# Rotary halves of the second mixer: exchanged by transfers within the on-chip memory instead of a product with a permutation matrix

## The chip, the cores and the metric

One Trainium2 chip, one core. The metric is the device time of the whole kernel in microseconds, as the median of several executions. TensorE multiplies matrices from the on-chip memory (SBUF) into the accumulator memory (PSUM, eight banks); VectorE (DVE), ScalarE (ACT) and GpSimd (POOL) work elementwise; SyncE (SP) and ScalarE issue transfers.

## The reference, cut to what matters

Three transformer blocks on 512 tokens of width 1024. The middle one's mixer has two halves that both start from the same normed input: a state space scan (16 heads in chunks) and a differential attention (8 heads of two 64-wide score maps each). The attention's queries and keys are turned by a rotary embedding before the scores:

```python
def rope(x, pos):                       # x: (batch, tokens, 16 heads, 64)
    half = x.shape[-1] // 2
    inv_freq = 10000.0 ** (-jnp.arange(half) * (2.0 / x.shape[-1]))
    ang = pos[:, :, None] * inv_freq
    cos, sin = jnp.cos(ang)[:, :, None, :], jnp.sin(ang)[:, :, None, :]
    x1, x2 = x[..., :half], x[..., half:]
    return jnp.concatenate([x1 * cos - x2 * sin, x2 * cos + x1 * sin], axis=-1)

def diff_attention_group(q, k, v, pos, layer, lambdas, subln):
    q, k = rope(q, pos), rope(k, pos)
    ...
        p1 = masked_softmax(q1 @ k1.T * scale, mask)
        p2 = masked_softmax(q2 @ k2.T * scale, mask)
        return (p1 - lam * p2) @ v
```

The third block's attention has a rotary part 32 wide, done in the same manner with its own matrix; it stays as it is but for the numbers of its semaphores.

## The kernel before, in words

Everything is laid out with features on the 128 partitions and the 512 tokens along the free dimension. Each engine runs one program in the order in which it is written; the engines meet by semaphores. Weights stream in panels of 128x1024 through five buffers: SP loads a panel, ScalarE casts it to its high part (`hi_to`, L1296), GpSimd subtracts to get the low part (L588), and TensorE multiplies in three rounded products for each pair of 128-row tiles (`units`, L617 to L619; 8 such steps make a projected tile 128x512).

The attention's queries and keys are projected in four parts p = 0 to 3, each of four tiles (`dqk0` to `dqk3`, tile n goes to `QD[p][:, n, :]`) and a value panel (`dv0` to `dv3`). Each tile holds two 64-wide heads, so its partitions are four groups of 32: first half, second half, first half, second half. ScalarE copies a finished tile out of its bank (`copy_dqkv`, L1566). TensorE then multiplies it by the matrix `rot64`, which exchanges the groups in pairs and changes the sign of one of each (`rotate`, L908, full fp32, into bank 2). VectorE does `rope` in three operations: bank 2 times the sine table (L2264), the tile times the cosine table (L2266), and their sum (L2267).

None of this is a stage by itself. The projection is filling that TensorE does between the steps of two other loops:

- the scan, 32 steps (`SSM_FILL`): in step s TensorE does half of the filling, the decay terms of step s + 1 (`segments`, L935 and L937, into banks 4 and 5), the other half, then the output products of step s (L958). `segments(s + 1)` waits until ScalarE's exponentials of step s (L1580) have read the banks. VectorE multiplies the exponentials by the masked products (L2295). In every fourth step VectorE also gates the output (`gate_y`, L2277 and L2280) or splits it into rounded parts (`split_y`, L1856, L1857, L1862). Parts 0 and 1 are projected here.
- the attention, 32 steps (`DIFF_FILL`): scores of step c + 1 (`scores`, L978, and the mask, L966) wait until the exponentials of step c (L1600) have read their banks; the exponentials wait for the maxima (L2310, L2311); probabilities are scaled (L2344 to L2347) and turned (L1022). Parts 2 and 3 and the first output projection (`out2a`) are projected here.

The patterns say how many fill steps TensorE takes in each loop step, a `rotate` counting as one. `steps_done` works out from the same numbers in which loop step a tile is finished (`DONE_SSM`, `DONE_DIFF`); ScalarE and VectorE use those tables to place their copies and rotations. In loop step s ScalarE does the exponentials of s (in the attention they were done in the step before) and then copies the tiles finished in step s - 1, casts a panel, and goes on to the exponentials of the next step; VectorE does its products of step s, then `gate_y` or `split_y`, then the rotations of the tiles listed for step s - 1. In the attention, VectorE does the rotations before the maxima of step s + 1.

Of the kernel before, what the change touches and what calls it, by code (L numbers as in the profile page):

```python
# [15 lines left out]
P = 128  # L16
# [119 lines left out]
for _name, _n in LATE:  # L136
# [2 lines left out]
NL = _at  # L139

CONSTS = [
    ("ident", 128), ("ones", 128), ("after", 128), ("upto", 128), ("rot64", 128), ("rot32", 128),
    ("pool_inv", 64), ("eps", 1), ("freq64", 1), ("freq32", 1),
]
CCOL = {}
_at = 0
# [24 lines left out]
def constants():  # L171

    i = np.arange(P)
    c = {}
    c["ident"] = np.eye(P)
    c["ones"] = np.ones((P, P))
    c["after"] = (i[:, None] > i[None, :]) * 1.0
    c["upto"] = (i[:, None] <= i[None, :]) * 1.0
    c["neg_keep"] = (i[:, None] >= i[None, :]) * -BIG
    c["neg_future"] = (i[:, None] > i[None, :]) * -BIG  # L180
    c["chunk_rows"] = ((i[:, None] % 64 == 63) & (i[None, :] < 64)) * 1.0
    rot = np.zeros((P, P))
    for m in range(P):
        rot[m + 32 if m % 64 < 32 else m - 32, m] = -1.0 if m % 64 < 32 else 1.0
    c["rot64"] = rot
    rot = np.zeros((P, P))
    for m in range(P):
        rot[m + 16 if m % 32 < 16 else m - 16, m] = -1.0 if m % 32 < 16 else 1.0
    c["rot32"] = rot
    pos = np.arange(1, 17)  # L190
    c["pool_inv"] = np.tile(np.concatenate([1.0 / np.minimum(pos, w) for w in POOL_W]), (P, 1))
    c["eps"] = np.full((P, 1), EPS)
    f64 = (10000.0 ** (-np.arange(32, dtype=np.float32) * np.float32(2.0 / 64)).astype(np.float64)).astype(np.float32)
    f32 = (10000.0 ** (-np.arange(16, dtype=np.float32) * np.float32(2.0 / 32)).astype(np.float64)).astype(np.float32)
    c["freq64"] = np.tile(f64, 4)[:, None]
    c["freq32"] = np.tile(f32, 8)[:, None]
    c["head"] = (i[:, None] == 32 * np.arange(4)[None, :]) * 1.0
    c["pick"] = ((i[:, None] % 32 == np.arange(16)[None, :]) & (i[:, None] < 96)) * 1.0
    return [np.concatenate([np.asarray(c[n], np.float32) for n, _ in names], axis=1) for names in (CONSTS, MASKS)]
# [56 lines left out]
def build(nc, xt, weights, vectors, late, consts, masks, w_gates, positions, out):  # L256

    ctx = ExitStack()
    with ctx:
# [192 lines left out]
        def lvec(name, i=0, n=1):  # L452
# [45 lines left out]
        s_zin, s_zs = sem("z_ready_for_silu"), sem("z_silu_ready")  # L498
        s_par, s_parx = sem("params_a"), sem("params_b")
        s_ang, s_sin = sem("angles_ready"), sem("sines_ready")  # L500
        s_qc, s_vd, s_rot, s_rotf, s_roped = (sem("qk_copied"), sem("v_copied"), sem("rotated"), sem("rotated_read"),
                                              sem("roped"))
        s_sc, s_mx, s_ex, s_pn, s_tr, s_pt, s_dv, s_osq, s_os, s_or, s_osp, s_og, s_yb = (
# [27 lines left out]

        def dqkv_items(p):
            name = f"dqk{p}"
            return [((name, 0), 8), ((name, 1), 8), (("rot", 4 * p), 1), ((name, 2), 8), (("rot", 4 * p + 1), 1),
                    ((name, 3), 8), (("rot", 4 * p + 2), 1), (("part", p), 12), (("rot", 4 * p + 3), 1),
                    ((f"dv{p}", 0), 4)]

        SSM_FILL = (3, 3, 3, 4)
        DONE_SSM = steps_done(dqkv_items(0) + dqkv_items(1), SSM_FILL, 32)
        DIFF_FILL = (12,) + (4, 5, 5, 5) * 7 + (5, 5, 5)  # L540
        _items = dqkv_items(2)
        _items.insert(1, (("cols", 0), 0))
        _items.insert(3, (("spread", 0), 0))
# [57 lines left out]
        def _(pe):  # L601
# [298 lines left out]
            products_bc(6)  # L900
            products_bc(7)

            def rotate(i):
                p, n = divmod(i, 4)
                pe.wait_ge(s_qc, i + 1)
                if i >= 1:
                    pe.wait_ge(s_rotf, i)
                mm_(ps[:, 2, :], con("rot64"), QD[p][:, n, :], start=True, stop=True).then_inc(s_rot, 1)  # L908

            def fill_dqkv(p):  # L910
                for n in range(4):
                    yield from units((f"dqk{p}", n), HX)
                    if p == 2 and n == 0:
                        norm_cols("gate", 7)
                    if p == 2 and n == 1:
                        norm_spread("gate", 7, RTG)
                    if n:
                        rotate(4 * p + n - 1)
                        yield
                for u, _ in enumerate(token_units((f"dv{p}", 0), HX)):  # L920
                    yield
                    if u == 11:
                        rotate(4 * p + 3)
                        yield

            def segments(s):
                pair, i = divmod(s, 4)
# [218 lines left out]

            def rotate_mla(i):
                if i:
                    pe.wait_ge(s_rotf, 16 + i)
                    pe.wait_ge(s_qc, 16 + i)  # L1150
                else:
                    pe.wait_ge(s_od, 6)
                    pe.wait_ge(bank_free[3], uses_through(3, "od_in"))
                mm_(ps[:, 3, :], con("rot32"), QR[:, i - 1, :] if i else OD[:, 9, :], start=True, stop=True
                    ).then_inc(s_rot, 1)

            def regroup(m):

                pe.wait_ge(s_gelu, m + 1)
                if m:  # L1160
                    pe.wait_ge(s_gs, 4 + m)
                else:
                    pe.wait_ge(s_rotf, 16 + 3)
                for i in range(TAPS):
                    for q in range(4):
                        mm = mm_(ps[32 * q:32 * q + 32, 3, CH * i:CH * i + CH], con("ident")[:, 32 * i:32 * i + 32],
                                 UU[:, 4 * m + q, :], start=True, stop=True)
                mm.then_inc(s_regrouped, 1)
# [118 lines left out]
        def _(act):  # L1287
# [260 lines left out]
            for c in range(6, 8):  # L1548
                copy_bc(c)

            def copy_dqkv(tile):
                name, t = tile
                if name in ("rot", "part", "spread"):
# [10 lines left out]
                if name == f"dqk{p}":  # L1564
                    bank = USE[tile][0][0]
                    link(nc.scalar.copy(QD[p][:, t, :], ps[:, bank, :]))  # L1566
                    act.sem_inc(bank_free[bank], 1)
                    act.sem_inc(s_qc, 1)
                else:
                    copy_rows(tile, lambda q: VD[p][:, q, :], s_vd)  # L1570
                hi_to(last_panel(name, t) + 5)
# [265 lines left out]
        def _(dve):  # L1837
# [410 lines left out]
            for t in range(8):  # L2248
# [5 lines left out]
                if t == 5:  # L2254
                    dve.wait_ge(s_sin, 1)
                    cosine(COS)
                    link(v.tensor_tensor(COS, COS, R, ALU.mult))
                    link(v.tensor_tensor(SIN, SIN, R, ALU.mult))

            def rope(i):  # L2260
                p, n = divmod(i, 4)
                x = QD[p][:, n, :]
                dve.wait_ge(s_rot, i + 1)
                link(v.tensor_tensor(ROPE_T, ps[:, 2, :], SIN, ALU.mult))  # L2264
                dve.sem_inc(s_rotf, 1)
                link(v.tensor_tensor(x, x, COS, ALU.mult))  # L2266
                link(v.tensor_tensor(x, x, ROPE_T, ALU.add))  # L2267
                dve.sem_inc(s_roped, 1)

            def ropes(tiles):  # L2270
# [240 lines left out]
            def rope_mla(i):  # L2511
                x = QR[:, i - 1, :] if i else OD[:, 9, :]
                tmp = S5T[0]
                dve.wait_ge(s_rot, 16 + i + 1)
                link(v.tensor_tensor(tmp, ps[:, 3, :], SINM, ALU.mult))
                dve.sem_inc(s_rotf, 1)
                link(v.tensor_tensor(x, x, COSM, ALU.mult))
# [252 lines left out]
```

## Time and profile before

| | us |
|---|---|
| median of three executions (2553.76 to 2554.94) | 2554.46 |
| the profiled execution, its own time | 2556.53 |
| span of its records | 2554.7 |
| TensorE busy | 2469.6 (97%) |
| VectorE busy | 1296.2 (51%) |
| GpSimd busy | 1061.4 (42%) |
| ScalarE busy | 868.2 (34%) |

The span runs from the first to the last record of the profiled execution; 1.8 us lie around it. Shares are means over stages with different limits. A busy TensorE is not one at its peak: matmuls are pipelined and their records overlap.

### The profile page before, as it was taken

Reading aid. Unit: us, or ns where it says so; the run is one execution under the profiler, and the core shown is the slowest. Engines: PE = TensorE matmul, PEld = TensorE weight load, DVE = VectorE, ACT = ScalarE, POOL = GpSimd, SP = SyncE. Lnnn points to the kernel's source line nnn. Section 1 sums busy time; section 2 is a strip of 40 time slices with the busy share of each in tenths; the row PEclk is TensorE's granted clock in tenths of the full one; section 3 lists DMA queues with packets and bytes.
Section 4 is the critical chain, followed back from the end, with each engine's and each line's share of the span. In section 5 each row is a group of like instructions: output and inputs, shape, how many; then the busy total and the mean of one; then the engine's idle time right before and its main releaser. Section 6 shows DMA issues by size and latency. Waiting matters only on the chain.

```text
span 2554.7 us, 30093 instructions
## 1 busy us (share of the span) xinstructions
PE 2469.6 (97%) x11694; PEld 1976.1 (77%) x11694; DVE 1296.2 (51%) x1928; ACT 868.2 (34%) x1360; POOL 1061.4 (42%) x830
## 2 busy tenths in 40 slices
PE   8999999999999999999989999999999889999998
PEld 6877667888888888876767778888888756788886
DVE  6336687533633321585757655586126865533301
ACT  4453246222322222244444433322224353322221
POOL 4323244654544445353222245455453222544442
PEclk9999999999999999999999999999998999999999
DMA  4212122322332333221111123332331112222232
GB/s 147 69 56 77 62 72 87 99 93 89 111 96 94 99 94 96 95 79 58 50 50 50 50 74 106 99 99 90 97 98 51 31 34 64 98 99 92 95 98 78
DMA packets 62573, 209.44 MB, mean 82 GB/s; under 512 B 6880, under 2 KB 9184, under 8 KB 62304
## 3 DMA queue, kind: packets, MB, share of 16 engines
q1 hardware_dynamic: 61424, 204.11, 25.0%
q10 hardware_dynamic: 1008, 3.41, 0.4%
q8 instruction: 93, 1.52, 0.2%
q14 instruction: 48, 0.39, 0.0%
HBM read 205.39 MB, written 2.10 MB: 81 GB/s over the span
## 4 chain that ended last, share of the span: by engine, by line
PE 86%; DVE 10%; ACT 2%; issue 2%; DMA 0%; DVEq 0%; ACTq 0%; SPq 0%
PE ps L617 24%; PE ps L619 24%; PE ps L618 24%; DVE T L2163 1%; PE ps L638 1%; PE ps L639 1%; PE ps L640 1%; PE ps L958 1%; PE ps L734 1%; ACT A L1600 1%; PE ps L725 1%; PE ps L991 1%; PE ps L978 1%; PE ps L812 1%; DVE small L2310 1%
## 5 line engine op out<-in xcount | busy, mean ns | idle before, releaser
L588 POOL TENSOR_TENSOR w_lo<-w_raw,w_hi 128x512 fp32r<-128x512 f32 (+4 forms) x822 | 1051.6, 1303 | 1454.9 <-ACT w_hi L1296 1454.7
L617 PE MATMUL ps<-H,w_hi 128*128 128x512 f32 x1880 | 756.5, 402 | 22.6 <-DVEq L1858 11.7
L619 PE MATMUL ps<-H,w_lo 128*128 128x512 f32 x1880 | 738.0, 393 | 0.0
L618 PE MATMUL ps<-H,w_hi 128*128 128x512 f32 x1880 | 737.2, 392 | 0.0
L1296 ACT CAST w_hi<-w_raw 128x1024 fp32r<-128x1024 f32 (+4 forms) x411 | 402.9, 984 | 523.7 <-DMA w_raw<-in_weights_dram 517.4
L617 PEld LDWEIGHTS ps<-H,w_hi 128*128 128x128 f32 x1880 | 356.1, 189 | 115.6 <-issue 24.4
L617 PE MATMUL ps<-split,w_hi 128*128 128x512 f32 x1034 | 411.5, 398 | 6.8 <-issue 3.3
L619 PEld LDWEIGHTS ps<-H,w_lo 128*128 128x128 f32 x1880 | 355.7, 189 | 75.8
L618 PEld LDWEIGHTS ps<-H,w_hi 128*128 128x128 f32 x1880 | 356.3, 190 | 73.2 <-issue 2.6
L619 PE MATMUL ps<-split,w_lo 128*128 128x512 f32 x1034 | 403.7, 390 | 0.0
L618 PE MATMUL ps<-split,w_hi 128*128 128x512 f32 x1034 | 403.5, 390 | 0.0
L1881 DVE TENSOR_TENSOR T<-ps,R 128x512 f32<-128x512 f32 x164 | 113.4, 691 | 411.7 <-PE ps L619 407.2
L617 PEld LDWEIGHTS ps<-split,w_hi 128*128 128x128 f32 x1034 | 194.5, 188 | 55.5 <-issue 11.7
L619 PEld LDWEIGHTS ps<-split,w_lo 128*128 128x128 f32 x1034 | 194.5, 188 | 40.9
L618 PEld LDWEIGHTS ps<-split,w_hi 128*128 128x128 f32 x1034 | 194.7, 188 | 40.3 <-issue 1.7
L1888 DVE TENSOR_TENSOR X<-X,ps 128x512 f32<-128x512 f32 x48 | 33.0, 687 | 332.4 <-PE ps L619 330.8
L1310 ACT ACTIVATE SQ<-X 128x512 f32<-128x512 f32 x49 | 31.0, 632 | 211.3 <-DVEq L1890 198.6
L1483 ACT ACTIVATE T<-T 128x512 f32<-128x512 f32 x66 | 41.7, 632 | 170.9 <-DVEq L2130 170.9
L2133 DVE TENSOR_TENSOR T<-T 128x512 f32<-128x512 f32 x66 | 78.3, 1186 | 9.7
L638 PE MATMUL ps<-w_hi,H 128*128 128x256 f32 x256 | 78.3, 306 | 0.0
L639 PE MATMUL ps<-w_lo,H 128*128 128x256 f32 x256 | 72.4, 283 | 0.0
L640 PE MATMUL ps<-w_hi,H 128*128 128x256 f32 x256 | 72.2, 282 | 0.0
(405 smaller groups left out, 2401.1 us busy)
## 6 DMA issues: line engine op xcount, KB each, us to landing
w_raw<-in_weights_dram SPq DMA_DIRECT2D x323, 512.0 KB, 3.5
w_raw<-in_weights_dram SPq DMA_DIRECT2D x48, 448.0 KB, 3.2
w_raw<-in_weights_dram SPq DMA_DIRECT2D x22, 256.0 KB, 2.6
X<-in_xt_dram SPq DMA_DIRECT2D x4, 512.0 KB, 7.8
out_dram<-A SPq DMA_DIRECT2D x8, 256.0 KB, 2.1
w_raw<-in_weights_dram SPq DMA_DIRECT2D x12, 128.0 KB, 2.0
w_raw<-in_weights_dram SPq DMA_DIRECT2D x6, 192.0 KB, 2.3
A<-in_w_gates_dram ACTq DMA_DIRECT2D x1, 1024.0 KB, 4.9
```

The lines of the kernel that those rows point to most:

```text
L588: sub = nc.gpsimd.tensor_tensor(w_lo[:, p % NS, c], w_raw[:, p % NS, c], w_hi[:, p % NS, c].bitcast(F32), ALU.subtract)
L617: mm_(ps[:, bank, :], r(wh), xh, start=(k == 0), stop=False)
L618: mm_(ps[:, bank, :], r(wh), xl, start=False, stop=False)
L619: mm = mm_(ps[:, bank, :], r(wl), xh, start=False, stop=(k == kt - 1))
L638: mm_(o, xh, r(wh), start=(k == 0), stop=False)
L639: mm_(o, xh, r(wl), start=False, stop=False)
L640: mm = mm_(o, xl, r(wh), start=False, stop=(k == kt - 1))
L1296: nc.scalar.copy(w_hi[:, p % NS, 0:PSIZE[p]], w_raw[:, p % NS, 0:PSIZE[p]]).then_inc(w_hi_ready[p % NS], 1)
L1483: A_(T[:, j % 2, :], T[:, j % 2, :], ACT.Silu).then_inc(s_silu, 1)
L1881: link(v.tensor_tensor(dst, ps[:, bank, :], R, ALU.mult))
L1888: link(v.tensor_tensor(X[:, t, :], X[:, t, :], ps[:, bank, :], ALU.add))
L2133: link(v.tensor_tensor(T[:, 2 + q, :], T[:, 2 + q, :], T[:, q, :], ALU.mult))
```

## The change

The matrix `rot64` and the sixteen products are taken out. When ScalarE has copied tile i = 4p + n, it issues four transfers within the on-chip memory, each of 32 partitions by 512 tokens (64 KB), which write the tile with its halves exchanged into ROPE_T. Before, it waits until VectorE has finished `rope` of the tile before (`s_swapf`), because there is one ROPE_T. The sign goes into the sine table by a column of plus and minus one (`sign64`). `rope` waits for the four transfers instead of the product, and multiplies ROPE_T by the sine table in place. A rotation no longer counts as a fill step: both patterns are cut by one fill step in each fourth loop step, eight in all in each loop.

```diff
-            return [((name, 0), 8), ((name, 1), 8), (("rot", 4 * p), 1), ((name, 2), 8), (("rot", 4 * p + 1), 1),
-                    ((name, 3), 8), (("rot", 4 * p + 2), 1), (("part", p), 12), (("rot", 4 * p + 3), 1),
+            return [((name, 0), 8), ((name, 1), 8), (("rot", 4 * p), 0), ((name, 2), 8), (("rot", 4 * p + 1), 0),
+                    ((name, 3), 8), (("rot", 4 * p + 2), 0), (("part", p), 12), (("rot", 4 * p + 3), 0),
                     ((f"dv{p}", 0), 4)]
 
-        SSM_FILL = (3, 3, 3, 4)
+        SSM_FILL = (3, 3, 3, 3)
...
-        DIFF_FILL = (12,) + (4, 5, 5, 5) * 7 + (5, 5, 5)
+        DIFF_FILL = (12,) + (4, 5, 5, 4) * 7 + (5, 5, 4)
...
-            def rotate(i):
-                p, n = divmod(i, 4)
-                pe.wait_ge(s_qc, i + 1)
-                if i >= 1:
-                    pe.wait_ge(s_rotf, i)
-                mm_(ps[:, 2, :], con("rot64"), QD[p][:, n, :], start=True, stop=True).then_inc(s_rot, 1)
...
+            def swap_halves(p, t):
+                if p or t:
+                    act.wait_ge(s_swapf, 4 * p + t)
+                else:
+                    act.wait_ge(s_dtn, 1)
+                    act.wait_ge(s_csr, 1)
+                for b in range(4):
+                    other = 32 * (b ^ 1)
+                    act.dma_start(ROPE_T[32 * b:32 * b + 32, :], QD[p][other:other + 32, t, :]).then_inc(s_swap, 16)
+
             def copy_dqkv(tile):
...
                     link(nc.scalar.copy(QD[p][:, t, :], ps[:, bank, :]))
                     act.sem_inc(bank_free[bank], 1)
                     act.sem_inc(s_qc, 1)
+                    swap_halves(p, t)
...
-                    link(v.tensor_tensor(SIN, SIN, R, ALU.mult))
+                    link(v.scalar_tensor_tensor(SIN, SIN, con("sign64"), R, ALU.mult, ALU.mult))
...
             def rope(i):
                 p, n = divmod(i, 4)
                 x = QD[p][:, n, :]
-                dve.wait_ge(s_rot, i + 1)
-                link(v.tensor_tensor(ROPE_T, ps[:, 2, :], SIN, ALU.mult))
-                dve.sem_inc(s_rotf, 1)
+                dve.wait_ge(s_swap, 64 * i + 64)
+                link(v.tensor_tensor(ROPE_T, ROPE_T, SIN, ALU.mult))
                 link(v.tensor_tensor(x, x, COS, ALU.mult))
                 link(v.tensor_tensor(x, x, ROPE_T, ALU.add))
+                dve.sem_inc(s_swapf, 1)
                 dve.sem_inc(s_roped, 1)
```

`fill_dqkv` on TensorE loses its calls of `rotate` and the fill steps they made. The waits of the third block's rotation are renumbered, since `s_rot` and `s_rotf` now start at zero there.

## Rows read from the trace of the kernel before

**Rows 1.** The page: busy time by engine, share of the span, instructions.
```profile
PE 2469.6 (97%) x11694; PEld 1976.1 (77%) x11694; DVE 1296.2 (51%) x1928; ACT 868.2 (34%) x1360; POOL 1061.4 (42%) x830
```

**Rows 2.** Windows: scan, attention; stretch, length, five engines' busy time, clock, DMA.
```profile
1165.00:1286.00 121.00, 118.62 (x635) 81.22 (x633) 75.97 (x120) 55.44 (x100) 31.43 (x23) 1.00 0.15 49
...
1296.00:1420.00 124.00, 114.96 (x640) 87.46 (x640) 78.08 (x177) 58.12 (x142) 26.71 (x20) 0.96 0.14 43
```

**Rows 3.** Waits of TensorE: sum, times, longest; then single ones in brackets.
```profile
PEld ps L908 <- ACTq L1568: 1.6, 2, 0.8
...
1299.05 0.70 PE L978 MATMUL ps<-A 64*128 64x256 f32 x4 [3.03 <-ACTq L1602]
...
1321.75 0.49 PE L978 MATMUL ps<-A 64*128 64x128 f32 x4 [1.38 <-ACTq L1602]
...
1398.68 0.70 PE L978 MATMUL ps<-A 64*128 64x256 f32 x4 [1.88 <-ACTq L1602]
```

**Rows 4.** Records by line, ns min/median/max; two fp32 products, a rounded one, on the chain.
```profile
L908 PE MATMUL ps<-A,C_ x32: 590/592/1061, 1188.7 to 1419.2; 128*128 128x512 f32 x32
...
L2267 DVE TENSOR_TENSOR A<-A x16: 691/694/1704, 1194.2 to 1424.1; 128x512 f32<-128x512 f32 x16
...
1158.28 0.86 PE ps L889 x2
1159.14 0.23 PE ps L617
```

**Rows 5.** Timeline of the scan: exponentials, a cast, a subtraction, a rotation; start, duration.
```profile
1190.14 0.84 ACT L1580 ACTIVATE T<-ps,small 128x256 f32<-128x256 f32 x2 [0.50 <-PE ps L937]
...
1197.84 1.26 ACT L1580 ACTIVATE T<-ps,small 128x512 f32<-128x512 f32 x2 [3.51 <-PE ps L937]
...
1205.12 0.84 ACT L1580 ACTIVATE T<-ps,small 128x256 f32<-128x256 f32 x2 [2.75 <-PE ps L937]
...
1208.63 0.62 ACT L1580 ACTIVATE T<-ps,small 128x128 f32<-128x128 f32 x2 [1.40 <-PE ps L937]
...
1210.31 1.05 ACT L1296 CAST w_hi<-w_raw 128x1024 fp32r<-128x1024 f32 x1 [0.18 <-ACT A L1566]
...
1211.43 3.02 POOL L588 TENSOR_TENSOR w_lo<-w_raw,w_hi 128x512 fp32r<-128x512 f32 x2 [7.31 <-ACT w_hi L1296]
...
1211.75 0.69 DVE L2264 TENSOR_TENSOR A<-ps,A 128x512 f32<-128x512 f32 x1
...
1216.28 1.05 ACT L1580 ACTIVATE T<-ps,small 128x384 f32<-128x384 f32 x2 [2.06 <-PE ps L937]
```

**Rows 6.** Timeline: issues on ScalarE's queue; SP's loads, us to landing.
```profile
8.25 0.33 ACTq L1330 DMA_DIRECT2D C_<-in_consts_dram  x1
8.62 0.45 ACTq L1331 DMA_DIRECT2D A<-in_masks_dram  x1
...
9.20 0.63 ACT L1306 ACTIVATE ACC<-X 128x512 f32<-128x512 f32 x1
...
DMA to landing us min/median/max: 1.9/3.4/12.6
```

**Rows 7.** Timeline of the attention: steps 1 and 6.
```profile
1311.92 1.28 ACT L1557 ACT_TABLE_LOAD   x1
...
1313.65 0.58 ACT L1600 ACTIVATE A<-ps,small 128x384 f32<-128x384 f32 x1 [0.44 <-DVE small L2311]
...
1340.35 0.68 DVE L2264 TENSOR_TENSOR A<-ps,A 128x512 f32<-128x512 f32 x1
...
1345.37 0.69 ACT L1600 ACTIVATE A<-ps,small 128x512 f32<-128x512 f32 x1 [3.89 <-DVE small L2311]
```

**Rows 8.** Windows of TensorE: stretch, length, busy (records), granted clock, DMA share, GB/s.
```profile
1300.00:1308.00 8.00, 8.00 (x26) 0.57 0.20 66
1399.00:1404.00 5.00, 5.00 (x20) 0.66 0.37 110
1321.00:1330.00 9.00, 7.33 (x37) 1.00 0.19 58
```

## What the change does to the time: the prediction

> **What bounds the kernel now.** I read the page's totals first [rows 1]. TensorE is busy 97% of the span, VectorE 51%, ScalarE 34%. So work taken off TensorE is worth its own length where the engine never waits, and nothing where it already waits for somebody. Both things are found in the stage that the change touches, so I read it in stretches [rows 2]. In the scan (1165 to 1286 us) TensorE is busy 118.6 of 121 us. In the attention (1296 to 1420) it is busy 115.0 of 124, and its long waits there are for ScalarE's exponentials: 3.0, 1.4, 1.9 us [rows 3]. The reader should keep the two apart: the scan is bound by TensorE, the attention alternately by TensorE and by the round maxima (VectorE), exponentials (ScalarE), next scores (TensorE).
>
> **What is removed.** Sixteen products of 128x128 by 128x512 in full fp32, two records each. They overlap with neighbours, so the mean of one record (0.59 us) overstates them and I take the row of the chain in which two such records in a row hold 0.86 us [rows 4]. Bounds: 0.46 us if they went at the pace of the rounded products (0.23 us each in the same view), 1.18 us by two means. 16 x 0.86 = 13.8 us, half in the scan (6.9), half in the attention (6.9). With them go two waits for the copy of a tile, 1.6 us, in the scan [rows 3]. The patterns of filling lose one step a head there, as many as there were products, so no projection work is moved between engines; the last tiles of each part move at most one step.
>
> VectorE: the first of the three operations of `rope` read one operand from PSUM, in 0.69 us [rows 5]; the third, with both from SBUF, has a median of 0.69 and a maximum of 1.70 [rows 4], the latter where GpSimd was subtracting (in step 11 from 1211.43 to 1214.45 [rows 5]). Alone, the first stays what it was: three operations and the gaps between them are 2.25 us. Beside a subtraction it may now take 1 us more. (The Trainium skill, "SBUF — State Buffer", Who interferes with whom, says so: a two-input operation of VectorE with both inputs in SBUF contends with GpSimd's reads, and one with a single SBUF input doesn't. The trace agrees, 1.70 against 0.69.) The sign moved into the sine table swaps one operation for another of the same size, once: nothing.
>
> **What is added, and where.** ScalarE's queue gets, right behind the copy of each of the sixteen tiles, a wait and four transfers. Two prices.
>
> First, issuing. The rows that are nearest are ScalarE's own: two transfers were issued at 8.25 and 8.62 us, durations 0.33 and 0.45, and the next activation came at 9.20 [rows 6]. That is 0.33 us bare and 0.37 to 0.47 from one to the next. Both are of 128 rows, none of 32 within the on-chip memory; below, the price could be near nothing if the number of rows sets it; above it is 4 x 0.47 = 1.9 us. I take the nearest row, a little over its bare duration, as the cost of an instruction and not of bytes: 4 x 0.39 = 1.55 us for each tile, 25 us of ScalarE in all. The question is what they push. [...]
>
> Second, the wait. The one buffer ROPE_T is free only when `rope` of the tile before is over, and VectorE does that `rope` in the same step as ScalarE copies the tile (the schedule puts both at the step in which the tile is complete). So ScalarE, which used to go straight from the copy to the cast of the next weight panel, stands until VectorE has done its products of this step and the whole rotation. Behind it in the queue are the cast (1.05 us) and the exponentials of the next step, for which TensorE waits: `segments(s + 2)` may not overwrite its bank before exponentials s + 1 have read it.
>
> Scan, tile 3 of a part (step 11, and 27), from the start of its exponentials at 1208.63 [rows 5]. VectorE: products and `split_y`, then `rope` from 3.12 (1211.75); it takes 2.25 us to 5.37, since GpSimd's subtraction comes after the cast and so is later now. ScalarE: wait over at 5.45, four issues 7.0, cast 8.15, then the first exponential, 0.63: 8.8. TensorE wants that bank when? Exponentials s + 2 began at 1216.28, so 7.65 after; less the product that is gone (0.86) and 0.4 for the segment itself: 6.4. It waits 2.4 us.
> Tile 1 (step 6, and 22), from 1190.14 [rows 5]: `rope` starts at 1.35, ends 3.6, issues to 5.25, cast to 6.4, a square of 0.63, first exponential 7.4. Wanted at 7.7 - 0.69 (one unit less in the pattern) - 0.4 = 6.6: 0.8 us.
> Tile 2 (step 8, and 24), from 1197.84: `rope` 2.05 to 4.3, issues 5.95, cast 7.1, exponential 7.65; wanted at 7.28 - 0.17 - 0.4 = 6.7: 0.95 us.
> Tile 0 has no wait, since the `rope` before is long over; its 1.55 us fit into the 2 us that ScalarE idles there: nothing.
> Sum for two parts: 2 x (2.4 + 0.8 + 0.95) = 8.3 us, and 0.8 for products of VectorE that now meet GpSimd's subtraction (an estimate: of six such places nearly one is longer by 1.0 us, the maximum less the median in [rows 4]). Scan: -6.9 - 1.6 + 8.3 + 0.8 = +0.6 us.
>
> Attention. Here the wait itself is free: the maxima of the next step come behind the same `rope` on VectorE, and ScalarE's exponentials wait for them anyway. What is not free is that issues and cast, which ran beside the rotation, now follow it. Step 6 [rows 7]: `rope` began at 1340.35 and, with GpSimd beside it, the maxima let the exponentials go at 1345.37. Now `rope` ends at 1342.6 (no subtraction yet), the issues at 1344.25, the cast at 1345.4: even. Step 1 has no rotation but two table loads behind the cast, the last over at 1313.20; with the issues at 1314.75, so that the exponentials start 1.1 us later than at 1313.65. Gone through in the same way, tile 1 (whose `rope` moves a step forward) is 0.3 us later, tile 2 0.3, and the second part's four cancel: 1.7 us. Against it stand the eight products. Six of them (0.86 us each) lie in rounds whose length VectorE and ScalarE set, and turn into waiting; two, among the value filling of each part, are in steps where TensorE never waits: 1.7 us gained. Attention: 0.0.
>
> Landing is hidden: 1.9 us at least, 3.4 in the median from issue to landing [rows 6], and 4.4 us or more lie between a tile's last issue and its `rope` (least for tile 2 of the last part, whose `rope` comes in the very next step). Without that cover each microsecond late would be one of VectorE.
>
> **The clock.** The waits also cost afterwards. TensorE stood 3.0 us before 1299.05, and over the eight us from 1300 the mean granted clock was 0.57 (1.2 of 2.4 GHz for most of it): 8 x 0.43 = 3.4 us lost [rows 3, 8]. After 1.88 us of waiting before 1398.7 it was 0.66 over five us: 1.7 us. After 1.38 us before 1321.75 it stayed at 1.00. By my sums four new stands of 1.9 us or more arise (2.4 us for tile 3 of both parts of the scan; some 3 us in steps 2 and 6 of the attention, where the wait before 1321.75 and one of 1.0 us take up the delays and the product's time). If half of them bring the lower level at the mean price of 2.5 us: +5.0 us.
>
> Sum: +0.6 + 0.0 + 5.0 = **+5.6 us**. The profiled execution took 2556.5 (span 2554.7 and 1.8 around it), 2.1 above the median of 2554.46; so 2562.1 for a profiled one, **2560.1 us** by the median.
>
> **Rivals.**
> A, the forecast: holds at ScalarE eat the saving and some clock is lost; 2556 to 2566.
> B, no change: the same holds, but no new drop of the clock, 2554.5 + 0.6 = 2555.1. For it: 1.38 us left the clock alone; against it: 1.88 did not.
> C, faster: issues on ScalarE cost little. By the lower bound, near nothing, each tile's hold shrinks by up to 1.55 us: the scan's stalls become 0, 0 and 0.85, twice, 1.7 us, and 6.9 + 1.6 - 1.7 = 6.8 is gained; in the attention the delays go and up to four products' time stays, 3.4: together -10.2, 2544.3 us, with no drop of the clock. It decides from under about 0.15 us for an issue. Against it stand the issue rows, though none has this shape. [...]
> D, much slower: a shape of 32 rows costs more to issue (0.8 us each would add 1.6 us to each of some ten exposed tiles, +16, with the clock 2576), or landings come behind `rope`.
>
> **Numbers.** A measurement of this kernel can tell 0.2%, 5.1 us. Chances: A 0.45, B 0.20, C 0.17, D 0.18. Faster is C, 0.17. A lies around the line of 2559.6; two thirds of it, and D, are slower: 0.48. The rest, 0.35, is same. The range leaves out the far halves of C and D: 2548 to 2573; A's own is 2556 to 2566.
>
> **What would show it.** Right: ScalarE issues 64 transfers of about 0.35 us; the four of a tile start within 0.2 us of the end of the third operation of `rope`; in the scan new waits of TensorE at the segments' weight loads for the exponentials, some 8 us in six, the longest at steps 12 and 28; in the attention the waits at L978 for the exponentials grow by the products' time, with waits of 3 us in steps 2 and 6. Wrong: issues of 0.1 us (then C); no waits at the segments (ScalarE had more slack than I count); a `rope` that waits for its transfer; a clock without new drops (B).

## The result, and the profile after

| | before | after |
|---|---|---|
| median, us (four executions each) | 2554.11 | 2578.05 (2574.24 to 2582.54) |
| ratio | | 1.0107 [1.0088, 1.0127] |
| ratio, the change run again (e12_again) | | 1.0107 [1.0089, 1.0124] |
| the profiled execution, its own time | 2556.53 | 2574.24 |
| first output product of the scan to the first scores | 118.3 | 140.5 |
| first scores to the last product of `root_spread` | 208.4 | 215.3 |
| from there to the end | 1055.1 | 1046.3 |

The change makes the kernel slower by 1.1%. I had forecast 2560.1 us with a range to 2573; it ended 5 us above the range. The last three rows of the table cut the profiled execution into stretches. Of the 17.7 us between the two spans (2554.7 and 2572.4) the scan has +22.2 and the attention +6.9. What lies ahead of the scan is 2.6 us shorter, which is within its scatter: that stretch is all but the same work in the fourteen profiles of this study and ends at 1170.3 to 1177.5 us. The stretch behind the attention is 8.8 us shorter; nothing ties that to the change, see the last section.

The page after, busy time by engine and the shares of the chain; TensorE's share fell by one point [rows 1], and an issuing line is on the chain with 1% of the span.

```profile
PE 2461.3 (96%) x11662; PEld 1971.9 (77%) x11662; DVE 1302.6 (51%) x1928; ACT 866.5 (34%) x1360; POOL 1059.4 (41%) x830
...
PE ps L615 23%; PE ps L617 23%; PE ps L616 23%; ACTq L1544 1%; DVE T L2159 1%; ACT A L1596 1%; PE ps L636 1%; DVE T L2291 1%; PE ps L637 1%; PE ps L638 1%; PE ps L732 1%; PE ps L723 1%; DVE small L2306 1%; PE ps L757 1%; PE ps L810 1%
```

The line of the new transfers (L1544): duration of an issue in ns, smallest, median and largest, then issue to landing.

```profile
L1544 ACTq DMA_DIRECT2D A<-A x64: 514/612/616, 1177.8 to 1431.2; - x64
...
DMA to landing us min/median/max: 1.9/2.0/3.0
```

An issue holds ScalarE's queue for 0.61 us, where I had taken 0.39 (ScalarE's earlier ones were 0.33 and 0.45 [rows 6]). Landing is hidden, as forecast.

The same two stretches of windows as in [rows 2], and the waits of the scan and the attention (sum, times, longest):

```profile
1165.00:1286.00 121.00, 106.97 (x527) 72.65 (x527) 70.68 (x104) 46.48 (x86) 27.96 (x20) 0.93 0.20 59
...
1296.00:1420.00 124.00, 107.77 (x593) 82.74 (x594) 71.39 (x155) 52.78 (x125) 26.27 (x20) 0.94 0.20 60
```
```profile
ACT w_hi L1281 <- issue: 39.3, 8, 7.1
...
PEld ps L919 <- ACT T L1576: 16.9, 7, 4.6
...
PEld ps L962 <- ACTq L1598: 18.0, 14, 4.9
```

In the scan TensorE is busy 107.0 of 121 us where it was 118.6, and the clock is 0.93 where it was 1.00. Ahead of the segments (L919) it waits 16.9 us for ScalarE's exponentials (L1576); before there was no such wait. ScalarE in turn is held eight times ahead of a cast (L1281), 4.9 us in the mean, wait and issues together. (A stand of TensorE is counted in two ways below: "PEld" at the weight load ahead of the segments, which gives the sums and the longest, and "PE" at the product behind it, up to 0.5 us less, which gives the single ones.)

Tile 3 of the first part, which is step 11 of [rows 5], in the timeline after (ScalarE, VectorE, TensorE; start, duration, in brackets the idle time before):

```profile
1211.04 0.60 ACT L1576 ACTIVATE T<-ps,small 128x128 f32<-128x128 f32 x2
1211.92 0.59 ACT L1561 COPY A<-ps 128x512 f32<-128x512 f32 x1 [0.27 <-PE ps L617]
...
1214.14 0.69 DVE L2260 TENSOR_TENSOR A<-A 128x512 f32<-128x512 f32 x1
...
1215.59 0.69 DVE L2262 TENSOR_TENSOR A<-A 128x512 f32<-128x512 f32 x1
...
1216.37 2.44 ACTq L1544 DMA_DIRECT2D A<-A  x4
1218.85 1.04 ACT L1281 CAST w_hi<-w_raw 128x1024 fp32r<-128x1024 f32 x1 [6.35 <-issue]
...
1220.54 0.69 PE L919 MATMUL ps<-CS,CR 80*128 80x384 f32 x1 [3.06 <-ACT T L1576]
```

Read it downwards. ScalarE's copy is over at 1212.51. It then stands until `rope` of the tile before ends at 1216.28, issues from 1216.37 to 1218.81, casts to 1219.89, and only then does the exponential for which TensorE has stood 3.06 us. This is the forecast order of events; the forecast stand was 2.4. `rope` itself is here as fast as foreseen, 0.69 us for its first and third operation.

The clock of TensorE in windows of 4 us across three of the six stands (stretch, length, busy, granted clock, DMA share, GB/s):

```profile
1192.00:1196.00 4.00, 2.59 (x12) 0.95 0.26 64
1196.00:1200.00 4.00, 4.00 (x15) 0.63 0.00 0
...
1216.00:1220.00 4.00, 1.48 (x12) 0.93 0.27 66
1220.00:1224.00 4.00, 3.46 (x15) 0.50 0.00 0
1224.00:1228.00 4.00, 4.00 (x20) 0.71 0.00 0
...
1272.00:1276.00 4.00, 0.04 (x1) 0.76 0.27 66
1276.00:1280.00 4.00, 3.83 (x12) 0.50 0.00 0
```

With four of the six stands come 3 to 7 us at 1.2 GHz (a window of 0.50 is all at that level, one of 0.71 more than half of it); those that end at 1206.12 and 1264.54, of 1.74 and 1.21 us, have none. The fall can begin while TensorE still stands: it resumes at 1276.17, and the window up to 1276 already has 0.76. Over the whole scan of 140.5 us the granted clock is 0.91. That is up to 140.5 x 0.09 = 12.6 us lost, an upper bound, since a part of the low level lies in the stands themselves.

### The profile page after: what moved, and what is told of

Same layout as the page of the kernel before. It is cut to its first block, busy times and chain, and to the rows that moved or that the text cites. A ratio compares the mean times of both kernels' runs of the same rounds, so it can differ in the third digit from the quotient of the medians.

```text
span 2572.4 us, 30079 instructions
## 1 busy us (share of the span) xinstructions
PE 2461.3 (96%) x11662; PEld 1971.9 (77%) x11662; DVE 1302.6 (51%) x1928; ACT 866.5 (34%) x1360; POOL 1059.4 (41%) x830
## 4 chain that ended last, share of the span: by engine, by line
PE 80%; DVE 13%; ACT 3%; issue 2%; ACTq 2%; DMA 0%; DVEq 0%; SPq 0%
PE ps L615 23%; PE ps L617 23%; PE ps L616 23%; ACTq L1544 1%; DVE T L2159 1%; ACT A L1596 1%; PE ps L636 1%; DVE T L2291 1%; PE ps L637 1%; PE ps L638 1%; PE ps L732 1%; PE ps L723 1%; DVE small L2306 1%; PE ps L757 1%; PE ps L810 1%
## 5 line engine op out<-in xcount | busy, mean ns | idle before, releaser
L1281 ACT CAST w_hi<-w_raw 128x1024 fp32r<-128x1024 f32 (+4 forms) x411 | 402.8, 984 | 593.2 <-DMA w_raw<-in_weights_dram 516.4
```

The source lines that it names most:

```text
L1281: nc.scalar.copy(w_hi[:, p % NS, 0:PSIZE[p]], w_raw[:, p % NS, 0:PSIZE[p]]).then_inc(w_hi_ready[p % NS], 1)
```

## The experiments

Theory: three things stand in a row on ScalarE's queue between a copy and the next exponentials, the wait for `rope`, the four issues and the cast. The scan has a slack there; past it, each further microsecond is a stand of TensorE, and the stands bring the low clock. Rivals: (a) the wait alone costs it, (b) the issues alone, (c) the transfers disturb something else (SBUF, DMA queues), (d) removing the products is itself no gain, (e) the low clock has nothing to do with the stands.

All runs in one table; ratios are to the kernel before on the same chip, and go before the medians (e1 to e4, e5 to e8 and e9 to e12 each shared their executions of the kernel before, with medians of 2552.48, 2548.10 and 2553.09). Scan and attention are the two stretches of the table above, in one profiled execution; "stands" is TensorE's waiting ahead of the segments for the exponentials, with the longest. The change was profiled twice, and its scan took 140.5 and 143.4 us: differences of some 3 us between two scans are not told from scatter by one profile each.

| run | median | ratio [95%] | scan | stands, longest | clock in the scan | attention |
|---|---|---|---|---|---|---|
| before | 2554.11 | 1 | 118.3 | 0 | 1.00 | 208.4 |
| the change | 2578.05 | 1.0107 [1.0088, 1.0127] | 140.5 | 16.9, 4.6 | 0.91 | 215.3 |
| e1_neither | 2544.47 | 0.9976 [0.9960, 0.9992] | 113.8 | 0 | 1.00 | 203.9 |
| e2_wait | 2545.84 | 0.9985 [0.9971, 0.9999] | 119.2 | 3.9, 1.1 | 1.00 | 202.6 |
| e3_issue | 2549.08 | 0.9993 [0.9979, 1.0007] | 117.5 | 0.7, 0.2 | 1.00 | 208.6 |
| e4_sp | 2544.04 | 0.9968 [0.9951, 0.9985] | 113.7 | 0 | 1.00 | 208.8 |
| e5_castfirst | 2570.46 | 1.0083 [1.0065, 1.0101] | 138.2 | 16.8, 4.5 | 0.91 | 208.2 |
| e6_late | 2547.43 | 0.9990 [0.9976, 1.0005] | 114.4 | 0 | 1.00 | 211.0 |
| e7_one | 2550.03 | 1.0001 [0.9986, 1.0016] | 123.2 | 6.9, 2.1 | 0.99 | 202.1 |
| e8_scan | 2571.44 | 1.0091 [1.0073, 1.0110] | 140.7 | 17.0, 4.6 | 0.92 | 208.8 |
| e9_fill | 2577.24 | 1.0094 [1.0080, 1.0108] | 136.3 | 8.4, 2.6 | 0.98 | 216.3 |
| e10_half | 2558.49 | 1.0019 [1.0009, 1.0028] | 128.5 | 10.7, 3.3 | 0.96 | 206.4 |
| e11_shapes | 2544.46 (one) | | 116.5 | 0 | 1.00 | 209.1 |
| e12_again | 2581.23 | 1.0107 [1.0089, 1.0124] | 143.4 | 18.3, 4.6 | 0.90 | 215.3 |

### Neither part, each part alone

e1_neither has no transfers and no wait. The exchange is left out: `rope` multiplies the tile itself by the sine table, in three operations as before.

```diff
             def swap_halves(p, t):
-                if p or t:
...
+                return
...
-                dve.wait_ge(s_swap, 64 * i + 64)
-                link(v.tensor_tensor(ROPE_T, ROPE_T, SIN, ALU.mult))
+                link(v.tensor_tensor(ROPE_T, x, SIN, ALU.mult))
```

> Leaves out the exchange of the halves: no transfers, no wait on ScalarE, rope multiplies the tile itself by the sine table. Theory 1 (what costs is that ScalarE stands behind the wait and then behind four issues, in series, ahead of the cast and the exponentials): the saving of the product shows, 6.9 + 1.6 us in the scan and 1.7 to 3.4 in the attention, some 10 us faster than before, 2544 us (2540 to 2549). Theory 2 (VectorE and GpSimd collide more, since the first operation of rope now has both inputs in SBUF, and the product's time would not come back anyway): 2554 or more. Theory 3 (the schedule with rotations one step earlier costs by itself): 2560 or more.

e2_wait is the same, with ScalarE's wait put back behind the copy (`act.wait_ge(s_swapf, 4 * p + t)`), still without transfers.

> Leaves out the exchange, but ScalarE still waits at each tile until rope of the tile before is over. Theory 1: the wait alone fits into ScalarE's slack but for tile 3 of a part in the scan (0.9 us twice) and pushes the cast behind the rotation in the attention: 2 to 5 us above the kernel with neither, 2546 to 2551 us, still faster than before. If the wait is the whole cause: 2570 or more.

e3_issue has the 64 transfers but no wait for `rope`. The transfers' result is not used; `rope` takes its first operand from the tile, into another buffer.

```diff
-                    act.wait_ge(s_swapf, 4 * p + t)
+                    act.wait_ge(s_swap, 64 * (4 * p + t))
...
-                link(v.tensor_tensor(ROPE_T, ROPE_T, SIN, ALU.mult))
+                link(v.tensor_tensor(ZT, x, SIN, ALU.mult))
...
-                link(v.tensor_tensor(x, x, ROPE_T, ALU.add))
+                link(v.tensor_tensor(x, x, ZT, ALU.add))
```

> Leaves out the use of the transfers: ScalarE issues the same 64 transfers without waiting for rope (only for the landing of the ones before, long over), rope multiplies the tile itself by the sine table. Theory 1: 16 x 2.45 us of ScalarE's queue run beside VectorE's work, as the cast did; the scan has no stall, the attention 2 to 6 us: 2546 to 2553 us. If the price of the issues is the whole cause: 2565 or more.

Measured: 2544.47, 2545.84 (0.2 us below its range) and 2549.08. Taking the products out is worth 0.24% [0.08, 0.40], some 6 us, and the fastest executions differ by as much (2542.0 before, 2535.8 here); rival (d) falls. Over e1_neither the wait costs 1.4 us and the issues 4.6, neither beyond the intervals; both together (the change) cost 33 by the ratios (1.0107 - 0.9976). So (a) and (b) fall as sufficient causes. The scan shows the same: +5.4 and +3.7 us alone, +26.7 together.

### The same work elsewhere

e4_sp is the whole change, with the wait and the transfers in SP's program instead of ScalarE's, behind the load of the fifth panel after the tile's last.

```diff
             for p in range(2, PANELS):
                 panel(p)
+                if p in swaps:
+                    q, t = swaps[p]
+                    sp.wait_ge(s_qc, 4 * q + t + 1)
+                    if q or t:
+                        sp.wait_ge(s_swapf, 4 * q + t)
...
+                    for b in range(4):
+                        other = 32 * (b ^ 1)
+                        sp.dma_start(ROPE_T[32 * b:32 * b + 32, :], QD[q][other:other + 32, t, :]).then_inc(s_swap, 16)
...
             def swap_halves(p, t):
-                if p or t:
...
+                return
```

> The whole change with a right output, but the four transfers of a tile are issued by SP, behind the weight panel that goes out when the tile is complete; the wait for rope of the tile before stands on SP too. Theory 1: ScalarE is free again, so the time is that of the kernel with neither, plus at most a little for landings: 2543 to 2550 us, some 0.3% faster than before. If transfers within the on-chip memory disturb by their traffic, or landings are late for rope: above 2560. SP's next panel waits for the next tile, some 9 us later, so the weights should not be late.

2544.04, as fast as without any transfer. SP's issues take as long as ScalarE's did:

```profile
L583 SPq DMA_DIRECT2D A<-A x64: 507/591/1456, 1179.8 to 1401.1; - x64
```

They move the same bytes between the same places. Rival (c) falls: the transfers cost nothing that the medians or the scan (113.7 against 113.8 us) show where nobody stands behind them. The attention is 4.9 us longer than in e1_neither in the two profiles, with the clock at 0.95 against 0.97; why it fell more often there I have not followed.

e8_scan leaves parts 0 and 1 (the scan) on ScalarE and gives parts 2 and 3 (the attention) to SP.

> The whole change, right output; ScalarE issues and waits for the two parts projected in the scan only, SP for the two in the attention. Theory 1, read from the profiles: the loss lies in the scan (first output product to first scores: 140.5 us in the changed kernel, 118.3 before, 113.7 with SP), the attention loses 7: 2568 to 2573 us. If the attention is where it is lost: below 2558.

1.0091: of the distance from 0.9968 to 1.0107, 0.0123 is the scan's. The 0.0016 left for the attention (some 4 us) are within the intervals; the profiles say 215.3 - 208.8 = 6.5, and both profiles of the change have 215.3.

e6_late leaves everything on ScalarE, but the wait and the issues of a tile come behind the exponentials that follow, not ahead of them.

```diff
-                    swap_halves(p, t)
+                    pending.append((p, t))
...
                        bias=CN[:, i, 2 * pair + a:2 * pair + a + 1]).then_inc(s_e, 1)
+                swap_pending()
```

> The whole change, right output; ScalarE issues a tile's four transfers behind the exponentials of the next step, when rope of the tile before is over. Theory 1: the issues (2.45 us) remain on ScalarE, the wait costs nothing: as issues alone, 2549 us (2544 to 2556). If 39 us of issues on ScalarE cost by themselves wherever they stand: 2565 or more.

2547.43 and no stand in the scan, with the same engine, the same wait and the same 64 issues. It is the place in the queue that costs. All of the cost may not be gone: e4_sp is 0.2% faster still, with intervals that just overlap.

### The order within the row

e5_castfirst puts the cast ahead of the wait and the issues; these stay ahead of the exponentials.

```diff
                     act.sem_inc(s_qc, 1)
+                    hi_to(last_panel(name, t) + 5)
                     swap_halves(p, t)
```

> The whole change, right output; on ScalarE the cast of the next panel stands before the wait and the four issues instead of behind them. Theory 1 (a series on ScalarE between copy and next exponentials): the series is 1.15 us shorter at each tile, six stalls of the scan fall from 18 us to some 7 and fewer of them lower the clock: 2560 us (2553 to 2566). If only wait plus issues count and the cast is hidden anyway: 2574 or more.

1.0083, 2570.46: a miss, between the range (to 2566) and the rival (from 2574). Taking 1.05 us of cast out of the row should have shortened each stand; they stayed at 16.8 us in all. (The small gain on the change, whose interval overlaps, lies by the profiles in the attention: 208.2 us against 215.3.) The timeline of tile 3 shows where it went:

```profile
1213.84 0.59 ACT L1561 COPY A<-ps 128x512 f32<-128x512 f32 x1 [0.28 <-PE ps L617]
1214.61 1.05 ACT L1281 CAST w_hi<-w_raw 128x1024 fp32r<-128x1024 f32 x1 [0.18 <-ACT A L1561]
...
1215.73 3.01 POOL L586 TENSOR_TENSOR w_lo<-w_raw,w_hi 128x512 fp32r<-128x512 f32 x2 [8.02 <-ACT w_hi L1281]
...
1216.05 1.55 DVE L2261 TENSOR_TENSOR A<-A 128x512 f32<-128x512 f32 x1
1217.63 1.66 DVE L2262 TENSOR_TENSOR A<-A 128x512 f32<-128x512 f32 x1
1219.33 0.69 DVE L2263 TENSOR_TENSOR A<-A 128x512 f32<-128x512 f32 x1
...
1220.11 2.44 ACTq L1544 DMA_DIRECT2D A<-A  x4
1222.65 1.27 ACT L1577 ACTIVATE T<-ps,small 128x512 f32<-128x512 f32 x2 [7.00 <-issue]
```

The earlier cast lets GpSimd start its subtraction earlier, beside `rope`. The rotation takes 1216.05 to 1220.02, 3.97 us, where the change had 2.14 (1214.14 to 1216.28): 1.8 us more in front of the issues against 1.05 less behind them. (The Trainium skill, "SBUF — State Buffer", Who interferes with whom, has VectorE's operations with both inputs in SBUF contend with GpSimd; the two of 1.55 and 1.66 us beside the subtraction agree, against 0.69 without it.) The other places agree: at the five that still stand, one or two of the three operations take 1.55 to 1.80 us; at the sixth, tile 2 of the first part, the subtraction starts only at 1205.10 and `rope` ends undisturbed at 1205.33, and the stand of 1.74 us is gone.

### The dose

e7_one issues a single transfer of 128 rows behind the same wait, e10_half two of 64. In both the exchange is left out, every row goes to its own.

```diff
-                for b in range(4):
-                    other = 32 * (b ^ 1)
-                    act.dma_start(ROPE_T[32 * b:32 * b + 32, :], QD[p][other:other + 32, t, :]).then_inc(s_swap, 16)
+                act.dma_start(ROPE_T, QD[p][:, t, :]).then_inc(s_swap, 16)
```

> Leaves out the exchange: one transfer of 128 partitions instead of four of 32 for each tile, the wait as in the change. Tells what an issue costs by its shape: if it costs what the long ones cost (0.33 to 0.45 us), the price lies in the 32 rows; if 0.6, in a transfer from and to the on-chip memory. Theory 1: the series is 1.8 to 2.1 us shorter, only tile 3 still stalls in the scan (1.4 us twice): 2550 us (2546 to 2557).

> Two transfers of 64 rows in place of four of 32, behind the same wait; the exchange is left out (each row goes to its own row). The dose between one transfer (2550, stands of 6.9 us in the scan) and four (2578, 16.9 us). If what counts is the length of wait, issues and cast in a row beyond a slack, two issues of 0.5 us give stands of 9 to 11 us in the scan, the clock at 0.97, and 2554 to 2561. Rival, short rows of 32 are what costs and not the number of issues: as with one transfer, 2548 to 2552.

With 0, 1, 2 and 4 issues behind the wait the stands in the scan are 3.9, 6.9, 10.7 and 16.9 us, the clock 1.00, 0.99, 0.96 and 0.91, and the ratio 0.9985, 1.0001, 1.0019 and 1.0107. A tile's issues hold the queue 0, 0.47, 1.12 and 2.45 us. The stands grow by 13.0 us for 2.45: that is 5.3 stands that take each microsecond in full, and six there are. The last step, 1.12 to 2.45, adds 6.2 us of stands and 12.0 to the scan, and the granted clock takes up to 12.6 us where it took 128.5 x 0.04 = 5.1. In e7_one I had expected a stand at tile 3 alone; there were eight waits, 2.1 us the longest.

e11_shapes measures the issue by itself, for five shapes, without the wait for `rope` (the exchange is left out of the result, as in e3_issue).

> No wait for the rotation; behind each copied tile transfers of different shapes: four of 32 rows exchanged, four of 32 rows straight, two of 64, one of 128, and twice four of 16 rows. The exchange and the rotation's use of it are left out. If an issue's price is one of an instruction: about 0.5 us for the first of each group and 0.6 for those behind it, whatever the shape. Rival, by rows or descriptors: 16 rows cheaper than 32 and those cheaper than 64. Second rival, the exchange costs: straight rows about 0.5 where exchanged ones take 0.6. Time 2545 to 2552.

ScalarE's timeline: four exchanged rows of 32, four straight, two of 64, one of 128, and four of 16 rows.

```profile
1178.22 2.54 ACTq L1547 DMA_DIRECT2D A<-A  x4
...
1189.28 2.63 ACTq L1547 DMA_DIRECT2D A<-A  x4
...
1197.30 1.17 ACTq L1547 DMA_DIRECT2D A<-A  x2
...
1207.26 0.49 ACTq L1547 DMA_DIRECT2D A<-A  x1
...
1236.32 2.47 ACTq L1547 DMA_DIRECT2D A<-A  x4
```

One takes 0.49 us, two 1.15 to 1.17, four 2.4 to 2.6, whether of 16 rows or 32, exchanged or straight. The price is one of the instruction, and in a row each further one costs more than the first (0.49, then 0.61 to 0.66). Both rivals by shape fall. (Single issues took up to 1.5 us in e3_issue, e4_sp and e11_shapes; in the change none took over 0.62.) The time, 2544.46 us in one execution, is 0.5 below the range.

### The clock

e9_fill is the change, with 49 products laid by TensorE into the six places where it stands; their result is thrown away.

```diff
+            WARM = {7: 4, 9: 5, 12: 11, 23: 4, 25: 14, 28: 11}
...
                 run(fill, n // 2)
+                for _ in range(WARM.get(s, 0)):
+                    mm_(ps[:, 2, :], r(HX[0](0))[:, 0:P], r(HX[0](0)), start=True, stop=True)
                 if s + 1 < 32:
                     segments(s + 1)
```

> The change as it is, with 49 products of 128x128 by 128x512 (0.23 us each, result thrown away, into the bank that the removed products used) laid by TensorE ahead of the six segments at which it stood, a little fewer in each than fill the stand. If part of the loss is the clock that falls to 1.2 GHz after the stands (about 12.6 us in the scan), it comes back in the scan (granted clock from 0.91 to 0.97 or more), a part of it being lost again as waiting, since a faster TensorE comes earlier to the exponentials: 2562 to 2571. Rival, the low clock comes by itself or the stands cost nothing beyond their length: the products only take the place of the waiting, time as the change, 2575 to 2582.

> The change itself once more, beside the three others on one chip, as their yardstick: ratio 1.008 to 1.012, 2572 to 2581.

TensorE's windows in e9_fill, first around a stand of 2.18 us that was left (it ends at 1213.38), then where one of 4.13 us had been:

```profile
1212.00:1216.00 4.00, 2.60 (x8) 0.72 0.08 19
1216.00:1220.00 4.00, 4.00 (x19) 0.85 0.00 0
1220.00:1224.00 4.00, 4.00 (x32) 1.00 0.41 135
...
1276.00:1280.00 4.00, 4.00 (x17) 1.00 0.09 27
1280.00:1284.00 4.00, 3.02 (x15) 1.00 0.20 49
```

The clock in the scan is 0.98, and falls there only behind the one stand that stayed long. Rival (e) falls: the five other places, filled with work so that at most 0.95 us of standing is left, have no drop. But the time, 2577.24 us, is a miss: it lies in the rival's range, 2575 to 2582, and not in mine, 2562 to 2571. By the clock alone 143.4 x 0.10 - 136.3 x 0.02 = 11.6 us came back in the scan against e12_again on the same chip. Stands and products together took 8.4 + 49 x 0.23 = 19.7 us where the stands alone had been 18.3, 1.4 more. The scan got shorter by 7.1, so some 3 us went into other waits that I did not follow. Of the whole kernel, 2577.24 against 2581.23, the two intervals overlap: that the scan gains some 7 us from the clock rests on one profile of each, and the medians don't show it.

The two profiles of the change show why a drop is worth less than its length. At tile 1 of the first part TensorE stood 1.41 us in one (it ends at 1195.34) and 1.39 in the other. Only in the first did the clock fall, and there the next stand was 1.74 us; in the other:

```profile
1199.93 0.50 PE L919 MATMUL ps<-CS,CR 80*128 80x512 f32 x1 [1.39 <-ACT T L1576]
...
1210.71 0.58 PE L919 MATMUL ps<-CS,CR 80*128 80x256 f32 x1 [3.30 <-ACT T L1576]
```

From stand to stand it is 10.78 us in both. While ScalarE sets the time, a TensorE at full clock only arrives earlier at the next wait. I take the clock as a part of the loss that is real and smaller than the stands; how much smaller stays open.

## Why the prediction was wrong

**What was right.** ScalarE's row of wait, issues and cast, and TensorE's wait behind it, are as described: the issues start 0.09 us after the end of `rope` (tile 3 above); TensorE stands for the exponentials at six places in the scan, for tiles 1 to 3 of both parts; tile 0 does not wait; landing is hidden; new stands bring the lower clock. The rise in the scan has the forecast cause (e2_wait, e3_issue, e4_sp, e6_late).

**The step that failed first: "First, issuing".** I took 4 x 0.39 = 1.55 us a tile from two issues of 128-row loads; it is 2.45. 0.9 us more at six exposed places is 5.4 us, which takes the 8.3 of stands to 13.7. Even my upper bound of 1.9 was short, and rival D, which had 0.8 us for an issue and 2576, came nearest, for a reason that does not hold (not the 32 rows, e11_shapes, but several issues in a row): its number was luck. The two nearest rows were different instructions, and I had read the gap from one to the next but not that of a queue of four. By itself this step gives 2560.1 + 5.4 = 2565.5 us, still within the range; it took the next two as well.

**The second: each tile's stand taken alone.** Measured were 16.9 to 18.3 us. That is 3 to 5 us more than 13.7. One place where they come from is tile 2 of the second part. The row of tile 1 has put off the exponentials of the step before (128 wide, at 1264.14), and with them VectorE's products, so that when the next exponentials start, at 1265.19, VectorE still has `split_y` and that step's products ahead of `rope`:

```profile
1265.19 1.27 ACT L1576 ACTIVATE T<-ps,small 128x512 f32<-128x512 f32 x2 [0.45 <-PE ps L921]
...
1266.92 0.59 ACT L1561 COPY A<-ps 128x512 f32<-128x512 f32 x1 [0.46 <-PE ps L617]
...
1269.88 0.68 DVE L2260 TENSOR_TENSOR A<-A 128x512 f32<-128x512 f32 x1
...
1272.11 2.44 ACTq L1544 DMA_DIRECT2D A<-A  x4
1274.59 1.04 ACT L1281 CAST w_hi<-w_raw 128x1024 fp32r<-128x1024 f32 x1 [7.08 <-issue]
...
1276.17 0.58 PE L919 MATMUL ps<-CS,CR 80*128 80x256 f32 x1 [4.13 <-ACT T L1576]
```

`rope` starts 4.69 us after those exponentials, where the undisturbed trace had 1.94 (I had read 2.05). I had 0.95 us of stand for tile 2; it was 4.13. I had also named tile 3 (steps 12 and 28) as the longest, and this one was.

**The third: the clock.** Forecast +5.0 for four stands of 1.9 us or more of which half would tell. In the scan alone the granted clock gives up to 12.6 us: four drops where I had counted two candidates there, and three of them cost 3.4 us (by their windows) where I had 2.5. In the attention it is 0.94 where it was 0.98, 12.9 us against 4.2, 8.7 more. So by the granted clock the term is some 21 us at most where I had 5.0. By e9_fill about 7 us of the scan's length come back when most of the low clock goes, so the bound overstates what the drops are worth, but even that is more than I had for the whole kernel.

**The attention.** Forecast 0.0, measured +6.9 by the profiles; against e1_neither it is +11.4. Its waits of TensorE for the exponentials are 18.0 us. I had forecast waits of some 3 us in steps 2 and 6. The one of step 6 ends at 1369.08 and is 1.64. The one of step 2 ends at 1342.94 and is 4.51, but it is no sign of the row on ScalarE, since e1_neither, with neither wait nor transfers, stands as long ahead of the same product:

```profile
1310.63 1.82 DVE L2252 TENSOR_TENSOR A<-A 128x512 f32<-128x512 f32 x1
1312.49 1.67 DVE L2253 TENSOR_TENSOR A<-A 128x512 f32<-128x512 f32 x1
...
1318.55 0.80 PE L962 MATMUL ps<-A 64*128 64x128 f32 x4 [4.96 <-ACTq L1591]
```

It comes with the removal. The first `rope` of the attention has moved a step forward, ahead of VectorE's maxima for the exponentials that TensorE waits for. In the kernel before it came behind them, at 1323.31, and the stand was 1.38 us [rows 3]:

```profile
1323.31 0.69 DVE L2264 TENSOR_TENSOR A<-ps,A 128x512 f32<-128x512 f32 x1
```

My sum had one such move, at 0.3 us. In e1_neither the rotation also takes 4.2 us there beside GpSimd's subtraction; in the change, where the cast and so the subtraction come behind `rope`, 2.1. The other long stand of the change, 3.30 us ahead of 1425.26, is at the product that had 1.88 before [rows 3], and 1.09 in e1_neither. Both have a low clock about them. What of the +11.4 is the issues' price and what the clock is not told apart.

**The removal.** Forecast -8.5 in the scan and -1.7 in the attention; e1_neither shows -4.5 and -4.5 by the profiles. The sum was right within 1.2 us, its distribution was not; that is luck.

In the sum the scan has -4.5 for the removal and +26.7 for wait and issues together, clock included (forecast -8.5 and +9.1, and a share of the clock's 5.0). Rival C, cheap issues, has its version in e4_sp, where issues are dear but hold nobody: 0.9968 [0.9951, 0.9985], where its 2544.3 us is 0.9960. That is faster than both kernels compared.

## What to carry to other kernels

Before giving an engine that also computes a DMA to issue, list what stands behind it in its queue and who waits for that; price each issue at what a row of them took here, 0.6 us, and do not put a wait, several issues and a cast in a row ahead of what a bound engine needs. Two additions that are each absorbed by the same slack may not be absorbed together: find the slack in the trace and compare it with their sum. If the work must stay on that engine, move it behind the critical instruction (e6_late) or to an idle queue (e4_sp). Once one stand arises, don't take later ones from the undisturbed order. And when work is taken out of a pattern, look at what its removal moves on the other engines: a kernel with the removal alone (e1_neither) tells it apart from what is added.

## What the runs showed of the hardware

An issue of a transfer within the on-chip memory held its queue 0.47 to 0.51 us alone, and 0.61 us in the median in a row of four on ScalarE, nearly so on SP (0.59). Two of 64 rows took 1.12 to 1.17 together. 16 or 32 rows of 2 KB, exchanged or straight, made no difference. Its landing took 2.0 to 2.3 us in the median.

Of the stands in the scan, those of 1.1 us at most (e2_wait) left the clock at 1.00; one of 1.41 us (it ends at 1195.34 in the change) was followed by 0.63 over 4 us, while the next, of 1.74, was followed by 1.00, and so was the stand of 1.39 at the same place in e12_again; one of 2.18 (e9_fill) had 0.72 and 0.85 about it. In the attention before 1.38 had left it alone [rows 3, 8]. The length of a stand alone does not tell it.

The clock also fell where TensorE never stood. In the profile of the kernel before, far behind the mixers:

```profile
1925.00:1930.00 5.00, 5.00 (x26) 0.88 0.28 100
1930.00:1935.00 5.00, 5.00 (x22) 0.50 0.00 0
...
1945.00:1950.00 5.00, 5.00 (x21) 0.57 0.31 105
```

TensorE is busy in every microsecond and at 1.2 GHz for some 20 of them: 10 us lost. None of the other thirteen profiles is as long in the stretch from the attention to the end: they have 1046.3 to 1047.6 us there, this one 1055.1. So the 8.8 us by which this stretch is shorter after the change come from this drop. One profile of each kernel doesn't tell whether the change has any part in it; no row ties the two. The kernel before scatters from 2542.0 to 2558.6 over the 35 executions beside e1 to e4, with granted clocks from 0.991 to 0.984, and the medians contain such drops as often as they came. What makes the clock fall there stays open.
